# One list of weight loads in a mixture-of-experts decoder kernel, put in another order

## The reference, cut to what matters

```python
def block(args):
    tb, cb = args
    a = jnp.einsum('td,edf->tef', tb, w_g)
    u = jnp.einsum('td,edf->tef', tb, w_u)
    hh = jax.nn.silu(a) * u * cb[:, :, None]
    return jnp.einsum('tef,efd->td', hh, w_d)
```

## Time and profile before

| | us |
|---|---|
| median of 3 runs | 963.09 (959.80 to 964.55) |
| profiled execution, its own time | 962.18 |
| span of that execution | 960.3 |
| TensorE busy in the span | 853.5 (89%) |
| mean granted TensorE clock | 0.957 of full |

### The profile page before, as it was taken

The page is one execution under the profiler, slowest core; times in us unless marked ns, Lnnn a source line. Parts: engine busy times, 40 slices in busy tenths (PEclk is TensorE's granted clock), DMA queues, the critical chain, the costliest instruction groups (busy, mean ns, idle before and its releaser), DMA issues.

```text
span 960.3 us, 20077 instructions
## 1 busy us (share of the span) xinstructions
PE 853.5 (89%) x8672; PEld 677.6 (71%) x8672; DVE 531.5 (55%) x1066; ACT 392.5 (41%) x664; POOL 112.7 (12%) x167
## 2 busy tenths in 40 slices
PE   7999899999899998877889988999998999977875
PEld 7997687878786665554479966878787766645543
DVE  6567778566544444433464767875655445534434
ACT  6457757444512222111365566673444222211113
POOL 6700102120000000000035001022200000000000
PEclk9999999999999999888899998999999999989887
DMA  9974344474879999999994544446566999999993
GB/s 270 363 257 160 104 157 150 168 314 175 345 293 418 420 418 420 420 420 419 392 314 166 164 143 132 133 174 224 214 263 263 384 418 420 419 420 420 420 419 128
DMA packets 63726, 281.49 MB, mean 293 GB/s; under 512 B 5264, under 2 KB 7360, under 8 KB 39056
## 3 DMA queue, kind: packets, MB, share of 16 engines
q1 hardware_dynamic: 62288, 278.71, 74.9%
q0 software_dynamic: 800, 1.40, 0.9%
q10 hardware_dynamic: 544, 0.01, 0.0%
HBM read 279.05 MB, written 1.05 MB: 292 GB/s over the span
## 4 chain that ended last, share of the span: by engine, by line
PE 61%; DMA 18%; DVE 9%; issue 5%; ACT 3%; SPq 2%; POOL 1%; DVEq 0%; ACTq 0%; POOLq 0%
DMA late<-in_w_exp_down 11%; PE ps L420 11%; PE ps L422 11%; PE ps L421 11%; PE ps L706 8%; DMA ring<-in_w_exp_up 6%; PE ps L695 5%; PE ps L762 4%; PE ps L720 4%; DVE split_lo L1415 2%; SPq L332 1%; POOL wide L1306 1%; PE ps L712 1%; PE ps L415 1%; PE ps L520 1%
## 5 line engine op out<-in xcount | busy, mean ns | idle before, releaser
L1415 DVE TENSOR_TENSOR split_lo<-ring,split_hi 128x1024 fp32r<-128x1024 f32 (+1 forms) x144 | 194.4, 1387 | 57.4 <-ACT split_hi L935 52.7
L420 PE MATMUL ps<-split_hi,hT_hi 128*128 128x512 f32 (+2 forms) x416 | 162.3, 390 | 21.0 <-DVE split_lo L1415 11.5
L421 PE MATMUL ps<-split_lo,hT_hi 128*128 128x512 f32 (+2 forms) x416 | 159.2, 383 | 0.0
L422 PE MATMUL ps<-split_hi,hT_lo 128*128 128x512 f32 (+2 forms) x416 | 158.8, 382 | 0.0
L935 ACT ACTIVATE split_hi<-ring 128x1024 fp32r<-128x1024 f32 (+1 forms) x140 | 141.3, 1051 | 27.1 <-PE ps L422 25.9
L1781 DVE TENSOR_TENSOR br<-br,ps 32x64 f32<-32x64 f32 x256 | 54.9, 215 | 142.3 <-ACT br L1135 139.7
L1135 ACT ACTIVATE br<-ps 128x64 f32<-128x64 f32 x64 | 14.3, 223 | 264.5 <-PE ps L706 264.5
L420 PEld LDWEIGHTS ps<-split_hi,hT_hi 128*128 128x128 f32 x416 | 79.0, 190 | 40.5 <-DVE split_lo L1415 18.4
L422 PEld LDWEIGHTS ps<-split_hi,hT_lo 128*128 128x128 f32 x416 | 79.2, 190 | 14.8
L421 PEld LDWEIGHTS ps<-split_lo,hT_hi 128*128 128x128 f32 x416 | 79.3, 191 | 13.3
L695 PE MATMUL ps<-idx,wide 128*128 128x128 f32 x512 | 67.7, 296 | 17.4 <-DVE idx L1738 17.4
(11 more groups left out here) (250 smaller groups left out, 1298.4 us busy)
## 6 DMA issues: line engine op xcount, KB each, us to landing
ring<-in_w_exp_gate SPq DMA_DIRECT2D x54, 1024.0 KB, 22.2
ring<-in_w_exp_up SPq DMA_DIRECT2D x54, 1024.0 KB, 25.0
ring<-in_w_in SPq DMA_DIRECT2D x52, 1024.0 KB, 5.6
late<-in_w_exp_down SPq DMA_DIRECT2D x44, 1024.0 KB, 26.6
ring<-in_w_exp_down SPq DMA_DIRECT2D x20, 1024.0 KB, 26.8
late<-in_w_exp_gate SPq DMA_DIRECT2D x10, 1024.0 KB, 22.7
late<-in_w_exp_up SPq DMA_DIRECT2D x10, 1024.0 KB, 25.5
ring<-in_w_branch SPq DMA_DIRECT2D x8, 1024.0 KB, 4.9
```

The costliest lines, as they stand in the source:

```text
L420: mm(dst, st[0], mv[0], start=start, stop=False, skip_group_check=True)
L421: mm(dst, st[0], mv[1], start=False, stop=False, skip_group_check=True)
L422: return mm(dst, st[1], mv[0], start=False, stop=stop, skip_group_check=True)
L1415: V.tensor_tensor(half_view(split_lo[:, v % SPLITS, :], v), raw_half(v, l), half_view(split_hi[:, v % SPLITS, :], v).bitcast(F32), ALU.sub ...
```

## The change

Only the list `NEXT_LOADS` changes, for both layers. Before, the list runs pair e + 2, down e, pair e + 3, down e + 1. After, it runs down e, pair e + 1, down e + 1, pair e + 2. `FIRST_LOADS`, the places, the waits of each load and all work on the other engines are the same.

```diff
-NEXT_LOADS = [("gu", RP + k) for k in range(3)]
+NEXT_LOADS = [("gu", RP + k) for k in range(2)]
 for _e in range(RD, NE):
-    if _e + 2 < NE:
-        NEXT_LOADS.append(("gu", _e + 2))
     NEXT_LOADS.append(("d", _e))
+    if _e + 1 < NE:
+        NEXT_LOADS.append(("gu", _e + 1))
```

## The result

The changed kernel takes 969.52 us (median of 9 runs, 966.99 to 971.41), the kernel before on the same chip 963.09 us (9 runs, 959.80 to 964.91). The ratio is 1.0071, 95% interval 1.0059 to 1.0082: slower by 6.4 us. The forecast was 964.1 us, the range 961.0 to 968.6; the median lies 0.9 us above it. The profiled execution took 971.39 us with a span of 969.5, against 962.18 and 960.3 before: 9.2 us apart, so 2.8 of that belong to these two executions and not to the change.

A forecast was written before the change was run, and what follows sets the result against it. The prediction took the full DMA queue to set the pace in the later part of each expert stage. Order cost and clock gain cancelled; 0.5 us a layer for an idle gave 963.1 + 1.0 = 964.1 us, range 961.0 to 968.6.

The forecast's parts named there:

- T does not move: T, the last load landing of each layer's expert stage, stays put since the same 77 transfers are listed: cost nothing.
- the prediction's own sign: Profile after: T unchanged within 1 us in both layers; later by over 1 us would mean the queue ran dry.
- dry queue: Rival at the restart of loads: the queue empties, 1.4 us a layer, 2.8 in all, 965.9 us; chance 0.07.
- The waits for downs go, the waits for pairs stay: Sign in expert stages: PE's wait for downs near zero, that for pairs as long as before or longer, beginning earlier.
- The chain behind pair 31, step by step: End of layer 0: pair 31 lands at 465.8, gate_up 31 starts 465.9, down 31 ends 472.0, scatter starts 473.1.
- So the order costs 2.5 us a layer and the clock gives 2.55 back: sum 0 in both: Stage end, both layers: later pair 31 costs 2.5 us; down 31 and the last scatter at full clock give 2.55 back.
- the idle ahead of pair 30: PE idles 1.6 us before pair 30 and may meet the low clock: 0 to 1.2 us a layer, taken as 0.5.
- The rival with the low clock at the end: Gate_up 31 and what follows run at the low clock: 2.5 to 4.3 us a layer; chance 0.13 both, 0.17 one.
- The restart: Loads after pair 7: down 7 is issued later but in time by 0.9 us, so cost nothing; worst 1.4 a layer.
- No effect: Rival: landings do not follow the order of issue, pair 31 is not late, time stays 963.1 us; chance 0.05.
- faster: Rival at the stage ends: downs that land early remove PE's waits, 957.7 us; chance 0.05.

The follow-up runs named there:

- the new list with the old end: Changed list in both layers, but pairs 30 and 31 again ahead of downs 29, 30 and 31, against the kernel before: 962.79 us, 1.0003.
- two behind: Old list in both layers, but pair 31 between downs 29 and 30, so two transfers follow it, against the kernel before: 961.83 us, 0.9988.
- no filler at the turn: Kernel before without the 16 keep-warm matmuls between its layers, whose results nobody reads: 959.55 us, 0.9964 against the kernel before.
- filling moved: Extra unread matmuls at experts 11 and 15: 28 in the changed kernel, 963.81 us, 1.0014; 35 in the kernel before, 959.66 us, 0.9969.
- end-only: Old list in both layers, but pair 31 behind downs 29 and 30, one down behind it, against the kernel before: 969.04 us, 1.0072.
- one-layer kernels: New list in one layer, old in the other, against the kernel before: layer 0 alone 965.59 us, 1.0031; layer 1 alone 966.04 us, 1.0035.
- the pair with the clock held: Extra unread matmuls where PE waits near the stage end: changed kernel 961.20 us, 0.9985; kernel before 958.38 us, 0.9940, both against the kernel before.

## Why the prediction was wrong

**T does not move: right in layer 0, not in layer 1.** The queue ran at 419 GB/s as before, and no wait for a place appeared. In layer 0, pair 6's issue and T lie 471.6 - 272.9 = 198.7 us apart, 198.0 before. In layer 1 both executions of the changed kernel had T 1.5 to 2.3 us later than the two of the kernel before, measured from the layer's first gather, which by the prediction's own sign is more than nothing. It was no dry queue: the share at the restart is 0.99, and a little way ahead of T it falls early (0.69, shown above). Exactly the three profiles with such a late T (these two, and the new list with the old end) have landings out of the order of issue by 0.7 us or more in layer 1: a down landed up to 1.3 us ahead of the pair issued before it. The new list with the old end has the ratio 1.0003, and three others with the new restart in layer 1 don't have the late T. Why the landings of some executions come apart is open.

**The waits for downs go, the waits for pairs stay: right.** No row for downs against 2.0 us for those in `late`; for pairs 22.5 against 12.8 + 3.9 = 16.7 us over the same stretch.

**The chain behind pair 31, step by step: right.** It gave a scatter 473.1 - 468.3 = 4.8 us after T; at the full clock, and with PE free when pair 31 lands, it was 4.6 to 4.7.

**What failed is the step "So the order costs 2.5 us a layer and the clock gives 2.55 back: sum 0 in both".** The 2.5 is right. The 2.55, which counts 1.8 for the scatter and 0.8 for down 31, was to come back in both layers, 5.1 in all. The scatter's part came back in layer 1 alone (1.7 to 2.0 us), and that of down 31 was there in one of the two executions of the kernel before. The 2.55 rested on one execution, in which down 31 and the scatter behind it had met the low clock. The runs show three things in its place.

First, the low clock of down 31 was not the rule. In four other profiles with an old or nearly old end in layer 0 (before again, new list in layer 1 only, old end put back, two behind) down 31 took 1.07 us and the scatter started 2.3 to 2.4 us after T; in two (no filler at the turn, filling moved) it took 1.93 and 1.94, and the scatter started 3.2 us after T. The scatter itself met the low clock in 8 of the 12 last scatters with three transfers behind pair 31 and no filling near the end, and ran in 3.67 us in every one with fewer behind. That the new order would run it at the full clock was right. Second, in layer 0 the length of the scatter is off the path. In the profiles of before, after and the second execution of before, the next block of PE starts 6.3 to 6.4 us after the scatter's start, behind a pause, whether the scatter takes 3.67 or 5.66 us. So 1.8 of the 2.55 could not have come back there even had the first execution been typical. Third, the order brings low clock of its own. With fewer transfers behind them, pairs 29, 30 and 31 are what PE waits for close to the end; one of them can follow a long wait and run at the low level, as the earlier trace rows had shown for 416.14 and 445.90, and can delay the rest.

Stage by stage, as means of the two profiled executions of each kernel:

| us | before | after | more |
|---|---|---|---|
| start to first gather of layer 0 | 263.7 | 266.6 | 2.9 |
| first gather to T, layer 0 | 204.8 | 205.1 | 0.3 |
| T to the scatter's start, layer 0 | 2.7 | 5.1 | 2.4 |
| scatter's start to first L420 of layer 1 | 16.7 | 17.9 | 1.2 |
| first L420 to first gather, layer 1 | 250.6 | 250.4 | -0.2 |
| first gather to T, layer 1 | 204.5 | 206.4 | 1.9 |
| T to the scatter's start, layer 1 | 2.7 | 5.3 | 2.6 |
| scatter's start to the end | 14.4 | 12.5 | -1.9 |

Without the first row the sum is 6.3 us, and the change measures 6.4. So the price of 2.5 a layer is there (2.4 and 2.6: the bare 2.35, 0.4 to 0.6 for the idle ahead of pair 30, less 0.4 for the slow down 31 in one of two executions before). The clock gives 1.9 + 0.7 back instead of 5.1, and two terms that the sum put at nothing or left out have 3.1 together: the turn of the layers, and T of layer 1. Two executions of each do not tell which of these two is the rule. Over more kernels they spread otherwise. In five profiles with an old end or two behind and four with one behind, without added work on PE, these are the means:

| us | old end or two behind | one behind | more |
|---|---|---|---|
| scatter's start after T, layer 0 | 2.5 | 6.0 | 3.5 |
| T to first L420 of layer 1 | 19.4 | 23.0 | 3.5 |
| T of layer 1 to the end | 15.9 | 18.7 | 2.7 |

The last two rows sum to 6.2 us. Here three of the five that count as old in layer 1 have their last scatter at the full clock, so that what the clock gives back in layer 1 shows less, and the late chain of the end-only and one-layer kernels takes its place. What experiments show is this: the whole loss goes with the end of the list, the bare order accounts for 2.35 x 2 = 4.7 us at the scatter's start, and about 1.7 more is the net of what came back and what was lost elsewhere. That rest is not explained. The low clock is one candidate: the chains behind T are 0 to 2.5 us longer than 4.65. The turn of the layers is another, since the pair with the clock held and the pair with the filling moved, in which the second pause is gone, are both 0.45% apart, and the chains of the moved pair are just as long as the others. No run separates them.

**The rival with the low clock at the end was near in time and partly right in mechanism.** I gave it 970 us in both layers, 965.6 to 967.4 in one, with 0.13 and 0.17. Gate_up 31 at the low clock in both layers is what the end-only kernel shows, 3.64 us in each. In the profile after, it was gate_up 29 in layer 0 (3.64) and gate_ups 29 and 30 in layer 1 (2.91 and 3.50) that ran low. The argument against it, that the scatter of group 6 fills the time ahead of pair 31, held for the changed kernel; in the end-only kernel, with pair 30 further ahead, 3.83 us were left behind that scatter. So that the measured time is near this rival's is not because its mechanism was at work.

**The restart: right that it costs nothing the times show** (1.0003 with the old end), though its margin of 0.9 us was used up: the DMA share there is 0.99 at 400 and 407 GB/s instead of full.

**No effect, and faster: neither came, as forecast.** Pair 31 landed two transfers later against T than before, as its place in the list says, and in 29 of the 32 layers profiled no landing was out of the order of issue by more than 0.03 us; the three others are named above. Downs that land early bring nothing, since only down 31 counts for T.

What stays open: which execution meets which low stretch. What is shown is that it differs between executions. With PE kept busy ahead of pairs 29 and 30, gate_up 31 took 1.95 to 1.96 us behind waits of 0.1 to 0.4 us. Behind a wait of 2.5 us it took 3.56 in layer 0 and 1.95 in layer 1 of one and the same execution.

## What to carry to other kernels

At the end of a stage that waits for loads, count the work behind each landing, not the order of use. The last loads should be those with the least work behind them, and a load with more work behind it should stand ahead by at least the difference in transfers (here 7.2 - 2.3 = 4.9 us, two transfers). Before a lower clock seen in one execution is booked as a reserve to be paid from, look at a second execution, and ask of each stage whether the length of the slow work is on the path at all: here it was in layer 1 and not in layer 0.

## What the runs showed of the hardware that I had not expected

The low clock falls at different places in executions of one kernel. Down 31 took 1.82 us in one and 1.07 in the next behind the same idle of 1.5 us. Even ahead of the first expert the profiles make two groups: the load of pair 6 is issued at 270.2 to 270.5 us in six of sixteen profiles and at 272.2 to 273.6 in the ten others, old and new lists in both groups. For instance, from 103 to 118 us the second execution of the changed kernel has a mean granted clock of 0.76, the kernel with the old end put back 0.89, as have the five others of the first group. But one of the second group (the kernel before with its filling moved) has 0.95, so the clock there does not explain the groups alone. The kernel before was in the first group in both its profiles, the changed kernel in the second in both, so whether this goes by the execution or by the kernel is open. A single profile can be 2 to 3 us off by this alone.

TensorE pauses at the turn of the layers without waiting for any engine, shown as "issue": once until 6.2 to 6.4 us after the scatter's start (2.5 to 2.7 us where the scatter takes 3.67), and again about 6 us later (1.6 to 3.4 us). The second pause vanished when 28 or 35 small matmuls a layer were added at a quite different place in the program, and L420 came 13.6 and 14.1 us after the scatter's start in the two kernels with the filling moved, against 16.3 and 17.1 in the profiles of the kernel before and 18.2 and 17.5 in those of the changed one. The trace has a few packets of the queue for instructions near both pauses, and I read them as TensorE's program being fetched. No run separates that from other causes, so it is an explanation that was only argued. For timing experiments the runs suggest that an edit which adds instructions to an engine can gain 0.3 to 0.6% without doing anything for the work: that is what the moved filling gained in the two kernels. Both pairs with moved pauses were needed to see the order's own 0.45%.
